# Gate columns as fp32 matmuls inside the first key product, and the recurrence's scaled keys on ScalarE instead of GpSimd

## What is computed

```
h = rmsnorm(x, g1)
z = h @ w_in                       # 1024 x 8200, cut by columns into
(mq, mk, mv, mo, mi, mf, sb, sc, sx, dq, dk, dv, gt) = split(z)
ig = mi + b_if[0];  lf = log_sigmoid(mf + b_if[1])       # 4 heads: 8 gate columns
# mLSTM recurrence, per block of tokens:
s = (q @ k^T) * w                  # w = exp(dlog - mt)
num = s @ v + inter * (q @ C)
C_new = il * C + (wl * k)^T @ v    # wl = w[..., -1, :], the last row of w
n_new = il * n + sum(wl * k)
```

## Time and profile before

| | |
|---|---|
| median of 3 runs | 1013.2 us (1012.11 to 1013.21) |
| the profiled execution | 1012.78 us, of which 1011.0 us are the span from first to last instruction |
| TensorE busy | 980.3 us, 97% of the span |
| DVE / ACT / POOL busy | 684.7 / 464.0 / 161.3 us |
| mean granted TensorE clock | 0.989 of full speed |
| chain that ended last | PE 82%, DVE 7%, ACT 4%, issue 4% |

### The profile page before, as it was taken

How to read it: one execution, slowest core, us unless ns; L and a number is a source line. 1 busy time by engine, 2 the same in 40 slices (tenths; PEclk the granted TensorE clock), 3 DMA queues, 4 the chain that set the end, 5 groups by cost and what they waited for, 6 DMA issues and landing times.

```text
span 1011.0 us, 20145 instructions
## 1 busy us (share of the span) xinstructions
PE 980.3 (97%) x7816; PEld 959.4 (95%) x7816; DVE 684.7 (68%) x1170; ACT 464.0 (46%) x966; POOL 161.3 (16%) x341
## 2 busy tenths in 40 slices
PE   5999999999999999999999999999999999999996
PEld 4999999998999998999999999999999999999996
DVE  6877656578665898777775547777777777634341
ACT  5665545467554656555554434333344333322221
POOL 2000112120020312111012211211211111111010
PEclk9999999999999999999999999999999999999998
DMA  6523152355223232323335212222223222332302
GB/s 194 193 68 100 47 112 88 85 158 168 86 84 84 64 85 63 106 63 87 103 97 176 94 59 84 85 85 84 90 97 97 94 84 80 121 98 73 91 26 88
DMA packets 98069, 96.98 MB, mean 96 GB/s; under 512 B 4740, under 2 KB 93721, under 8 KB 97719
## 3 DMA queue, kind: packets, MB, share of 16 engines
q1 hardware_dynamic: 92879, 82.49, 27.8%
q10 hardware_dynamic: 3976, 10.36, 2.9%
q0 software_dynamic: 1120, 2.86, 0.8%
HBM read 88.38 MB, written 7.31 MB: 95 GB/s over the span
## 4 chain that ended last, share of the span: by engine, by line
PE 82%; DVE 7%; ACT 4%; issue 4%; DMA 1%; POOL 1%; ACTq 0%; DVEq 0%; POOLq 0%; SPq 0%
PE D L1626 43%; PE D L1658 28%; PE D L1643 3%; DVE w_l L1252 2%; ACT w_h L969 1%; PE X L1847 1%; PE X L1885 1%; DMA x_t<-in_x_prompt 1%; DVE acc L1592 1%; DVE ups L1582 1%; PE X L1779 1%; PE D L1743 1%; PE X L1793 1%; DVE f_x L1331 0%; PE X L1794 0%
## 5 line engine op out<-in xcount | busy, mean ns | idle before, releaser
L1252 DVE TENSOR_TENSOR w_l<-raw,w_h 128x512 fp32r<-128x512 f32 (+1 forms) x274 | 193.6, 725 | 117.6 <-ACT w_h L969 116.1
L1658 PE MATMUL D<-a_h,w_h 128*128 128x272 f32 x840 | 251.8, 300 | 3.4 <-ACT mqT L1085 1.5
L1658 PE MATMUL D<-a_h,w_l 128*128 128x272 f32 x840 | 244.4, 291 | 0.0
L1658 PE MATMUL D<-a_l,w_h 128*128 128x272 f32 x840 | 243.2, 290 | 0.0
L969 ACT ACTIVATE w_h<-raw 128x512 fp32r<-128x512 f32 (+1 forms) x274 | 164.0, 618 | 102.2 <-PE D L1626 75.7
L1658 PEld LDWEIGHTS D<-a_h,w_h 128*128 128x128 f32 x840 | 159.8, 190 | 6.1 <-ACT mqT L1085 1.7
L1658 PEld LDWEIGHTS D<-a_l,w_h 128*128 128x128 f32 x840 | 160.1, 191 | 0.0
L1658 PEld LDWEIGHTS D<-a_h,w_l 128*128 128x128 f32 x840 | 159.5, 190 | 0.0
L1626 PE MATMUL D<-h_h,w_h 128*128 128x272 f32 x704 | 145.9, 288 | 0.0
L1626 PE MATMUL D<-h_h,w_l 128*128 128x272 f32 x704 | 145.7, 288 | 0.0
L1626 PE MATMUL D<-h_l,w_h 128*128 128x272 f32 x704 | 145.1, 288 | 0.0
(11 more groups left out here) (331 smaller groups left out, 1701.8 us busy)
## 6 DMA issues: line engine op xcount, KB each, us to landing
raw<-in_w_in SPq DMA_DIRECT2D x64, 512.0 KB, 3.8
raw<-in_w_up SPq DMA_DIRECT2D x44, 512.0 KB, 4.3
raw<-in_w_down SPq DMA_DIRECT2D x16, 512.0 KB, 3.8
raw<-in_w_branch SPq DMA_DIRECT2D x12, 512.0 KB, 3.5
raw<-in_w_out SPq DMA_DIRECT2D x8, 512.0 KB, 4.5
raw<-in_w_down SPq DMA_DIRECT2D x8, 384.0 KB, 3.3
x_spill<-xT ACTq DMA_DIRECT2D x1, 2176.0 KB, 8.0
xT<-x_spill ACTq DMA_DIRECT2D x1, 2176.0 KB, 10.5
```

Of the source, the lines that this page charges most:

```text
L1252: v.tensor_tensor(split_view(w_l, g), whole_view(g), split_view(w_h, g).bitcast(F32), ALU.subtract)\
L1658: last = t.matmul(out, wt[:, k, :], x[:, left, k, :], start=w in (1, 2, 5) and k == i == 0, stop=k == KQ - 1 and i == 2, skip_group_check= ...
```

## The change

1. The gate product `("if", 0)` is no longer a unit of its own. The gate columns are copied once (ACT, two small copies) into a zeroed fp32 tile `gate_w`, and TensorE multiplies them in plain fp32 with `f_x` itself, two matmuls per block, ahead of the six matmuls of the same block of the key product `("mk", 0)`. All later units move one place forward.
2. The first two splits of the key weights (units 0 and 1) come before the norm on ACT and DVE.
3. The nine small loads are issued by ACT, behind `x_s`, in place of SP.
4. The scaled keys `kw` are made by ACT, four copies with a scale of one column, in place of one multiplication on GpSimd.
5. Where the two raw items of a pair lie in neighbouring slots, DVE makes the sums 7 and 5 in one instruction of 128 x 2 x 512.
6. The step `left 1` on DVE, which overwrites a part of `f_x`, waits for the gate product.

```diff
-        if kind == "if":
-            return [(("if", 0), 0, KD, 0)]
...
+    both = [q for q in pairs if ITEMS.index((q, 0)) % NRAW + 1 == ITEMS.index((q, 1)) % NRAW]
     for q in pairs:
         u6 = u_of(q, 6) - AHEAD
-        for w, e in ((7, u6 - 3), (6, u6 - 2), (5, u_of(q, 5) - AHEAD - 2), (4, u_of(q, 4) - AHEAD - 2)):
+        for w, e in ((7, u6 - 3), (6, u6 - 2), (5, u6 - 3 if q in both else u_of(q, 5) - AHEAD - 2),
+                     (4, u_of(q, 4) - AHEAD - 2)):
             T_MAKES.setdefault(e, []).append((q, w))
...
@@ SP: the nine small(...) loads are taken out; ACT, behind its load of x_s:
+            def small(dst, src):
+                act.dma_start(dst, src).then_inc(S["small_in"], 16)
+            small(small_a[0:8, :], blocks(norm1[0]))
...
@@ GpSimd
-            g.memset(gates_h[:, :, H:32].bitcast(F32), 0.0)
-            g.memset(gates_l[:, :, H:32].bitcast(F32), 0.0).then_inc(S["gates_zeroed"], 1)
+            g.memset(gate_w[:], 0.0).then_inc(S["gates_zeroed"], 1)
...
-                elif kind == "ml" and a[0] == "kw":
-                    u, c = a[1], ML_ORDER[a[1]]
-                    L = TILES[c][1]
-                    pool.wait_ge(S["ml_w"], u + 1)
-                    if u >= 1:
-                        pool.wait_ge(S["ml_num"], u)
-                    wait_drained(pool, block_of[("tokS", ("mk", 1))])
-                    g.tensor_tensor(kw[0:L], mk_tok[0:L, c], w_ml[0:L, :, L - 1:L].to_broadcast([L, H, P]),
-                                    ALU.mult).then_inc(S["ml_kw"], 1)
@@ ScalarE
+            act.wait_ge(S["gates_zeroed"], 1)
+            act.wait_ge(S["if_in"], 16)
+            for at_col, col in ((0, 0), (32, H)):
+                last = sc.activation(gate_w[:, :, at_col:at_col + H], raw_if[:, :, col:col + H], ACT.Copy)
+            last.then_inc(S["gates_ready"], 1)
             split(0)
+            split(1)
...
-                    for g in range(1, AHEAD):
+                    for g in range(2, AHEAD):
                         split(g)
...
+                    elif sub == "kw":
+                        act.wait_ge(S["ml_w"], u + 1)
+                        if u >= 1:
+                            act.wait_ge(S["ml_num"], u)
+                        wait_drained(act, block_of[("tokS", ("mk", 1))])
+                        for h in range(H):
+                            last = sc.activation(kw[0:L, h, :], mk_tok[0:L, c, h, :], ACT.Copy,
+                                                 scale=w_ml[0:L, h, L - 1:L])
+                        last.then_inc(S["ml_kw"], 1)
@@ VectorE
-                v.tensor_tensor(t_view(q, w), x, y, op).then_inc(S["t_ready"], 1)
+                if q in both and w == 7:
+                    if i:
+                        dve.wait_ge(S["wl_ready"], u_of(pairs[i - 1], 5) + 1)
+                    s0 = ITEMS.index((q, 0)) % NRAW
+                    b = raw[:, s0:s0 + 2, :].rearrange("p s (k f) -> p s k f", k=KQ)
+                    v.tensor_tensor(tw[:, 0:3:2, :].rearrange("p s (k f) -> p s k f", k=KQ), b[:, :, :, P:2 * P],
+                                    raw[:, s0, :].rearrange("p (k s f) -> p s k f", k=KQ, s=2), ALU.subtract)\
+                        .then_inc(S["t_ready"], 2)
+                elif not (q in both and w == 5):
+                    v.tensor_tensor(t_view(q, w), x, y, op).then_inc(S["t_ready"], 1)
...
                 elif kind == "norm" and a[0] == 0:
                     split(0)
+                    split(1)
                     wait_drained(dve, block_of[("rstd",)])
...
                     elif a[0] == 1:
                         dve.wait_ge(S["s_ready"], 3)
                         dve.wait_ge(S["al_ready"], KD)
+                        dve.wait_ge(S["dense_done"], block_of[("if",)] + 1)
@@ TensorE
+            def gates_and_wait(k):
+                n = block_of[("if",)]
+                if k == 0:
+                    pe.wait_ge(S["gates_ready"], 1)
+                pe.wait_ge(S["f_ready"], k + 1)
+                for half in range(2):
+                    last = t.matmul(banks(n)[0:36, half, 0:HALF], gate_w[:, k, :],
+                                    f_x[:, k, HALF * half:HALF * half + HALF], start=k == 0, stop=k == KD - 1)
+                if k == KD - 1:
+                    last.then_inc(S["dense_done"], 1)
+                pe.wait_ge(S["al_ready"], k + 1)
...
-                elif kind == "if":
-                    plain_product(n, lambda k: pe.wait_ge(S["al_ready"], k + 1))
                 elif kind == "mk":
-                    plain_product(n)
+                    plain_product(n, gates_and_wait if a[0] == 0 else None)
```

More of the change, by code:

```diff
@@ L316, in streaming_encoder_step @@
             else:
-                items = [u[0]] if kind != "if" else []
+                items = [u[0]]
             for it in items:
@@ L679, in wait_whole @@
             what, w = UNITS[g][0:2]
-            if g == 0:
-                eng.wait_ge(S["if_in"], 16)
-            elif what not in pair_no:
+            if what not in pair_no:
                 wait_item(eng, what)
@@ L939, in _ @@
             act.dma_start(x_s[0:TS, :], x_sample[0]).then_inc(S["xs_in"], 16)
+            def small(dst, src):
+                act.dma_start(dst, src).then_inc(S["small_in"], 16)
+            blocks = lambda ap: ap.rearrange("(j f) -> j f", f=P)
+            small(small_a[0:8, :], blocks(norm1[0]))
+            small(small_a[8:16, :], blocks(norm2[0]))
+            small(small_a[16:28, :], w_sc_conv[0].rearrange("t (j f) -> (t j) f", f=P))
+            small(small_a[28:36, :], state_conv[0, 0].rearrange("t (j f) -> (t j) f", f=P))
+            small(small_a[36:40, :], ml_norm[0])
+            small(small_a[40:41, :], da_norm)
+            small(small_b[0:2 * JU, :], state_ffn[0, 0].rearrange("t (j f) -> (t j) f", f=P))
+            fc = w_fconv[0].rearrange("t (j f) -> (t j) f", f=P)
+            small(small_c[0:66, 0, :], fc[0:66, :])
+            small(small_c[0:66, 1, :], fc[66:132, :])
             act.wait_ge(S["const_ready"], 7)
@@ L961, in split @@
                 wait_split_slot(act, g)
-                if g == 0:
-                    act.wait_ge(S["gates_zeroed"], 1)
-                    for at_col, col in ((0, 0), (32, H)):
-                        last = sc.activation(split_view(w_h, 0)[:, :, at_col:at_col + H], raw_if[:, :, col:col + H],
-                                             ACT.Copy)
-                    last.then_inc(S["wh_ready"], 1)
-                else:
-                    sc.activation(split_view(w_h, g), whole_view(g), ACT.Copy).then_inc(S["wh_ready"], 1)
+                sc.activation(split_view(w_h, g), whole_view(g), ACT.Copy).then_inc(S["wh_ready"], 1)
             def high_left(q):
@@ L1123, in _ @@
                         .then_inc(S["rows_act"], 2)
-                elif kind == "ml" and a[0] in ("w", "sq", "hm"):
+                elif kind == "ml" and a[0] in ("w", "kw", "sq", "hm"):
                     sub, u = a
@@ L1243, in split @@
                 dve.wait_ge(S["wh_ready"], g + 1)
-                if g == 0:
-                    dve.wait_ge(S["gates_zeroed"], 1)
-                    for at_col, col in ((0, 0), (32, H)):
-                        cols = slice(at_col, at_col + H)
-                        last = v.tensor_tensor(split_view(w_l, 0)[:, :, cols], raw_if[:, :, col:col + H],
-                                               split_view(w_h, 0)[:, :, cols].bitcast(F32), ALU.subtract)
-                    last.then_inc(S["wl_ready"], 1)
-                else:
-                    v.tensor_tensor(split_view(w_l, g), whole_view(g), split_view(w_h, g).bitcast(F32), ALU.subtract)\
-                        .then_inc(S["wl_ready"], 1)
+                v.tensor_tensor(split_view(w_l, g), whole_view(g), split_view(w_h, g).bitcast(F32), ALU.subtract)\
+                    .then_inc(S["wl_ready"], 1)
             def make_t(q, w):
```

21 lines of the change are left out of this document (4 added, 17 removed).

## The result

| | before | after |
|---|---|---|
| median of 22 runs each | 1012.7 us (1011.0 to 1015.1) | 1016.1 us (1012.7 to 1021.6) |
| ratio, 95% interval | | 1.004 (1.0024 to 1.0057) |
| the profiled execution | 1012.78 us, span 1011.0 | 1021.61 us, span 1019.8 |
| mean granted TensorE clock | 0.989 | 0.983 |

The change makes the kernel slower by 0.4%, 3.4 us. The prediction was 1012.3 us and no change; the median lies above its range, which ended at 1015.0. The single times of the changed kernel lie in groups that go with the granted clock: nine of 22 between 1012.7 and 1013.9 at 0.993 to 0.995, seven between 1020.8 and 1021.6 at 0.983, the rest between. The profiled execution is of the dearest group, so what follows explains its 8.8 us, and a part of that is not in the median.

The account below looks back on a forecast made before the run. TensorE, busy 97% of the span, was taken as the bound. Terms -0.75 - 0.93 + 0.45 + 0.35 = -0.88 us took 1012.78 to 1011.9, plus 0.4 for the median: 1012.3 us, no tellable change; range 1009.2 to 1015.0.

Parts of the forecast that it names:

- the start at -0.75 us: Start, gates inside the first key product: that product ends at 32.0 us instead of 32.75.
- All three signs of being wrong: First key product ending before 31 or after 33.5; PEclk near 0.5 beyond 20.5 us; work behind 60 us shifted over 1.5.
- First `f_x` at 16.2 behind two splits: Start, DVE: two key splits ahead of the norm move the first `f_x` from 14.87 to 16.2 us, +1.3 us.
- The small loads: Start, ACT's queue: issuing nine loads there costs +0.3 us, with 0 and +1.3 us as the ends.
- fp32 at 0.465 us per matmul: Gate product: price of a 36 x 272 fp32 matmul, scaled from 128 x 129 ones at 0.22 us; 0.93 us per block.
- A key group at 0.75 us behind fp32: First key product: six key matmuls take 0.75 us after a block's gates, making 1.68 us per block.
- Clock low until 19.9: Start, TensorE: the 1.2 GHz level lasts until about 19.9 us, rising at the same place as before.
- No new wait: Start to first Strassen product: ACT and DVE run 1.5 to 1.7 us later, yet TensorE waits nowhere new; cover thin.
- The keys, -0.93 + 0.45 + 0.35: Recurrence, `kw` on ACT: wait at u = 1 goes (-0.93 us), copies late at u = 4 (+0.45) and u = 0 (+0.35).
- Merged sums at nothing: DVE: one 128 x 1024 sum takes at most the 1.29 us of two, costed at nothing, covered by splits four units ahead.
- Rival B: Slower: narrow fp32 gates keep the clock low; two 3.4 us stretches, there or in the recurrence, give 1015.7 us; chance 0.14.
- The level: Whole kernel: the median was taken to lie 0.4 us above the profiled execution, turning 1011.9 into 1012.3 us.

Follow-up runs that it names:

- d_mix: Kernel before, with three fp32r gate matmuls put into the first key product's blocks, own banks, splits 0 and 1 ahead of the norm; 1012.0 us (before 1013.0).
- i_fill_after: Changed kernel plus six unused fp32 matmuls while TensorE waits for the first `f_x`; 1013.2 us (before 1012.6).
- g_own: Changed kernel with `kw` on GpSimd, the fp32 gate product whole ahead of the first key product, no split ahead of the norm; 1014.3 us (before 1012.6).
- a_kw: Kernel before, with only the scaled keys `kw` moved from GpSimd to ScalarE; 1012.3 us (before 1013.0).
- c_bank: Changed kernel with the gates' sums in a PSUM bank pair of their own (6 and 7); 1017.1 us (before 1013.0).
- h_fill_mix: d_mix plus eight unused fp32 matmuls while TensorE waits for the first `f_x`; 1009.4 us (before 1012.6).
- j_sums: Kernel before, with only the merged sums 7 and 5 added; 1013.6 us (before 1012.4).
- s_delay: Kernel before, with thirteen unused fp32 matmuls just ahead of the second key product as a pure delay; 1015.0 us (before 1012.4).
- b_start: Changed kernel with the scaled keys `kw` put back on GpSimd; 1015.65 us (before 1013.0).
- e_kw123: Kernel before, with the scaled keys on ScalarE at u = 1, 2 and 3 only; 1012.4 us (before 1012.6).
- p_fill: Kernel before, plus six unused fp32 matmuls while TensorE waits for the first `a_l`; 1012.6 us (before 1012.4).
- l_best: Kernel before, with fp32r gates inside the first key product, eight filling matmuls, keys on ScalarE at u = 1 to 3, separate sums; 1007.2 us (before 1012.4).

## Why the prediction was wrong, step by step

The step that failed is the first term of the sum, the start at -0.75 us. In the changed kernel's profile the second key product starts at 36.34 us and not at 32.0, so the term is +3.6. Three things in it were wrong: the price of a block (1.99 us for 1.68), the clock (low until 23.0 for 19.9) and the wait for a bank (0.62 us for none). Behind the start, the merged sums, which I had put at nothing, cost 1.1 us. All three signs of being wrong came: the first key product ended after 33.5, PEclk stayed near 0.5 beyond 20.5 us, and the work behind 60 us took 5.1 us more.

- **First `f_x` at 16.2 behind two splits**: right, 16.17 (my sum had used 16.5). The small loads: 0.07 us and not 0.3.
- **fp32 at 0.465 us per matmul**: it measured 0.52 (1.04 per block). The estimate of 0.50 us, from the four passes of the Trainium skill (FP8 and Floating Point Precision, TensorE Precision Notes) at the kernel's 0.125 us, is nearer than my row. The filling matmuls, fp32 of full width and side by side, took 0.45 us each (17.27 less 13.69, by eight), so rows 7 were right for those and wrong for narrow ones between fp32r.
- **A key group at 0.75 us behind fp32**: wrong, 0.95. The first and the last pair of the six take 0.35 us in place of 0.25, a cost of going from one kind to the other that I had at nothing. It is neither the width nor the wait at each block: d_mix changes between 36 and 128 columns and waits at each block too, all in fp32r, and its pairs take 0.25 us at every place. With the gates it makes a block 1.99 us and not 1.68, over seven blocks 2.2 us. This is the term of the sum that was mis-sized most.
- **Clock low until 19.9**: wrong in the profiled execution, 23.0. (A clock of 0.65 over the 3 us from 18 gives 20.1 for before, not 19.9.) I carried over before's stretch though TensorE's start sets the pace now. The end of the first key product was to be 32.0; it was 35.7. Of the 3.7 us the blocks make 2.2, and the clock, by difference, about 1.5.
- **"No new wait"**: wrong. I had followed the gates' drain on ACT, but not the bank pair that it frees: 0.62 us.
- **The keys, -0.93 + 0.45 + 0.35**: right in each mechanism. Between `mqT` and `dv_tok` the two executions without a fall, i_fill_after (keys on ScalarE) and g_own (on GpSimd), differ by 0.79 us: 0.93 gained, 0.19 lost at u = 0. At u = 4 another 0.4 is lost: in a_kw product 2 begins at 203.94 us, and at its pace it would have begun at 203.54. That makes -0.3 and not -0.13.
- **Merged sums at nothing**: wrong, +1.1 us, measured alone. I named "an urgent DVE operation behind it, 0.6 us later" and then counted on the cover of four units; that covers splits, not the maximum and the softmax behind it.
- **Rival B** had the sign and nearly the median (1015.7), with half of its reason: the start runs longer at the low clock, but not because of narrow fp32, since filling took it away. That its 3.4 us are also the 3.4 of the median is luck: the price of a block and the merged sums are in the one and not in the other.
- **The level**: I added 0.4 us because three runs of before had their median at 1013.2; over 22 runs it is 1012.7, so the median lies where the profiled execution does.
- **The range** took in one fall of the clock more or less, where the profile of the changed kernel has six after the start and before's has three. Before's 22 times spread over 4 us, those of the changed kernel over 9.

**What stays open** is what sets the number of falls behind the start. A fall costs 1.4 to 1.6 us between `mqT` and `dv_tok` (a_kw 109.60 with one, i_fill_after 107.96 with none, both with the keys on ScalarE). Neither the keys' engine nor the one delay that I tried explains the number. The traces do show where falls come. The 14 profiles have 39 falls between the start and 990 us, and each begins within 1.7 us behind the start of one of six pieces of work:

| TensorE's work at or just ahead of the fall | profiles with a fall there |
|---|---|
| u = 0, the fp32 matmuls with `kw` | after, c_bank, d_mix, h_fill_mix, j_sums, s_delay |
| u = 1, the fp32 scores (`mqT`, `mkT`) | before, after, a_kw, b_start, c_bank, e_kw123, h_fill_mix, j_sums, p_fill, l_best |
| u = 2, the same | after, c_bank, e_kw123 |
| u = 3, the same | before, after, d_mix, g_own, p_fill, s_delay |
| 375 to 388 us, the first matmuls behind the wait of 2 us for `wdT` | before, after, b_start, d_mix, g_own, h_fill_mix, p_fill, l_best, s_delay |
| 597 to 607 us, fp32 matmuls of one column (`mean_w`) | after, a_kw, b_start, e_kw123, g_own |

The changed kernel's profile has a fall at all six, i_fill_after at none. The last of the six, in a stretch of 3 us (the granted clock, 0.61, stands behind the busy times):

```profile
606.00:609.00 3.00, 3.00 (x18) 2.98 (x18) 1.22 (x7) 0.00 (x0) 1.18 (x1) 0.61 0.00 0
```

Why a place has a fall in one execution and not in another stays open.

Of the 3.4 us of the median, the merged sums make 1.1 and the keys -0.3. The start and the falls share the rest, about 2.6, and the runs do not divide it further, since both vary from run to run.

## What to carry to other kernels

A slower kind of work is free where its engine waits, and costs in full where its engine sets the pace; before moving a product to another place, ask who sets the pace there, and count the bank that its drain holds. Merging two operations saves time on their engine but pulls the second one forward, so look for what stands between them: here a maximum with a softmax behind it. And work of no use in an idle stretch of TensorE can pay where TensorE sets the pace right behind it, here 2.3 us for six to eight matmuls.

## What the hardware showed that I had not expected

The granted clock was 1.00 while TensorE finished the transposes of x. In the versions without filling it fell to 0.50, the 1.2 GHz level, at 14.9 us (s_delay) to 18.2 us (c_bank), after an idle time that had begun near 14, and was back at 20.1 us in b_start and at 23.0 us in the changed kernel's profile, with the same start of the program. Fp32 matmuls between fp32r ones cost 0.1 us at each change of kind. Behind the start the clock also fell while TensorE was busy without a break: it was busy for 3.00 of 3.00 us in the stretches at 0.55 and 0.52. A fall costs nothing where TensorE's waits take it up: before has one at 381 us and a_kw none, and both take 156.8 us from `wdT` to `tmp`; a_kw waits twice for DVE there, 0.35 and 0.36 us, where before does not. And this stretch, with some 1,200 matmul records, took 156.80 to 156.84 us in the eight versions with the sums apart and 157.87 to 157.91 in the six with merged sums, whatever the rest. A time between two waits is a far sharper measure of a part than the median of a whole kernel: for the same 1.1 us, the interval of j_sums reaches from 0.6 to 2.3.
